# Four-pick or two-pick groups in the expert gathers of a two-block transformer kernel

## What is computed

```python
q = (ht @ w_q).reshape(T, PEER_HEADS, 2, PEER_QDIM // 2)
s = jnp.einsum('thpd,pnd->thpn', q, sub_keys).astype(jnp.float32)
top_s, top_i = lax.top_k(s, PEER_TOPK)
...
best_s, best_j = lax.top_k(cand_s.reshape(T, PEER_HEADS, -1), PEER_TOPK)
experts = jnp.take_along_axis(cand_i.reshape(T, PEER_HEADS, -1), best_j, axis=-1)
gates = jax.nn.softmax(best_s, axis=-1)
...
act = jax.nn.gelu(jnp.einsum('cd,ced->ce', xc, u[ec]))
return jnp.einsum('ce,ced->cd', gc.astype(xc.dtype) * act, v[ec])
```

## Time and profile before

| | |
|---|---|
| median of 3 runs | 2549.35 us (2547.14 to 2553.7) |
| profiled execution, its own time | 2536.68 us |
| its span, first to last instruction | 2534.9 us |
| TensorE busy | 1432.2 us, 56% |
| VectorE busy | 1292.3 us, 51% |
| ScalarE busy | 420.5 us, 17% |
| GpSimd busy | 557.1 us, 22% |
| moved by DMA | 894.91 MB, mean 353 GB/s |
| gathers (L829) | 512, 536.90 MB |
| from the dot of pick 0 to that of pick 255, first and second PEER stage | 736.7 us and 733.8 us |

### The profile page before, as it was taken

How to read it: one execution, slowest core, us unless ns; L and a number is a source line. 1 busy time by engine, 2 the same in 40 slices (tenths; PEclk the granted TensorE clock), 3 DMA queues, 4 the chain that set the end, 5 groups by cost and what they waited for, 6 DMA issues and landing times.

```text
span 2534.9 us, 26747 instructions
## 1 busy us (share of the span) xinstructions
PE 1432.2 (56%) x10223; PEld 744.0 (29%) x10223; DVE 1292.3 (51%) x3307; ACT 420.5 (17%) x1218; POOL 557.1 (22%) x571
## 2 busy tenths in 40 slices
PE   6998666766797845442333333699674333233334
PEld 4665333433574623110000000465442100000000
DVE  2622000100465566877555555484766776555555
ACT  1152000000214312231100000123323231000000
POOL 1000000000001133333333333100333333433332
PEclk9999877888898978665555565899887655556556
DMA  9988999999984678888999999892798889999998
GB/s 388 407 254 343 427 429 429 428 429 427 331 336 169 223 295 344 335 339 326 379 388 390 393 391 387 337 371 93 309 377 330 322 324 366 386 388 406 392 398 338
DMA packets 147200, 894.91 MB, mean 353 GB/s; under 512 B 18460, under 2 KB 30588, under 8 KB 63868
## 3 DMA queue, kind: packets, MB, share of 16 engines
q0 software_dynamic: 73728, 536.90, 53.4%
q1 hardware_dynamic: 73340, 356.25, 35.5%
HBM read 889.68 MB, written 3.42 MB: 352 GB/s over the span
## 4 chain that ended last, share of the span: by engine, by line
DMA 37%; PE 29%; DVE 17%; issue 6%; POOL 6%; ACT 5%; SPq 1%; POOLq 0%; DVEq 0%; PEldq 0%; ACTq 0%
DMA sb_area<-in_peer_uv,sb_peer_e 22%; DMA sb_area<-in_moe_w_gu 13%; PE psum L2055 8%; POOL sb_area L829 6%; DVE sb_area L2841 5%; PE psum L1394 5%; PE psum L1403 3%; PE psum L1480 3%; PE psum L1694 2%; DVE sb_area L2816 2%; ACT sb_peer_e L1188 2%; DMA sb_area<-in_ada_w 1%; PE psum L1719 1%; PE psum L1984 1%; DVE sb_area L2753 1%
## 5 line engine op out<-in xcount | busy, mean ns | idle before, releaser
L2055 PE MATMUL psum<-sb_area 128*32 128x512 f32 x2048 | 450.6, 1009 | 877.0 <-DVE sb_area L2816 877.0
L829 POOL DMA_INDIRECT sb_area<-in_peer_uv,sb_peer_e x512 | 538.8, 1052 | 1199.7 <-PE psum L2055 822.5
L2841 DVE CUSTOM_DVE_ANT_0 sb_area<-sb_area 128x1024 f32<-128x1024 f32 x448 | 547.7, 1224 | 417.9 <-DMA sb_area<-in_peer_uv,sb_peer_e 408.6
L2055 PEld LDWEIGHTS psum<-sb_area 128*32 128x32 f32 x2048 | 77.1, 155 | 1207.8 <-DVE sb_area L2816 1022.1
L1694 PE MATMUL psum<-sb_area 128*32 128x256 f32 x2048 | 173.5, 513 | 129.7 <-DMA sb_area<-in_moe_w_gu 127.2
L2335 DVE COPY sb_area<-psum 128x128 f32<-128x128 f32 x32 | 9.3, 292 | 392.2 <-PE psum L1706 392.2
L1278 ACT ACTIVATE sb_small<-sb_small 128x4 f32<-128x4 f32 (+1 forms) x134 | 27.5, 205 | 1092.8 <-DVE sb_small L2841 1092.4
L1394 PE MATMUL psum<-sb_area 128*128 128x256 f32 x784 | 174.6, 384 | 4.6 <-DVE sb_area L2169 3.2
L807 POOL TENSOR_SCALAR_AFFINE_SELECT sb_area<-sb_area 128x256 f32<-128x256 f32 x1 | 0.4, 406 | 726.2 <-DVE sb_area L2639 726.2
L1394 PEld LDWEIGHTS psum<-sb_area 128*128 128x128 f32 x784 | 150.0, 192 | 28.6 <-DVE sb_area L2169 3.5
L2250 DVE SCALAR_TENSOR_TENSOR sb_area<-sb_area,sb_c_silu 128x2048 f32<-128x2048 f32 x49 | 115.2, 2350 | 70.6 <-DMA sb_area<-in_ada_w 68.6
(11 more groups left out here) (380 smaller groups left out, 1629.6 us busy)
## 6 DMA issues: line engine op xcount, KB each, us to landing
sb_area<-in_moe_w_gu SPq DMA_DIRECT2D x30, 4096.0 KB, 33.6
sb_area<-in_ada_w SPq DMA_DIRECT2D x72, 1024.0 KB, 12.9
sb_area<-in_moe_w_dn SPq DMA_DIRECT2D x32, 2048.0 KB, 24.2
sb_area<-in_peer_w_q SPq DMA_DIRECT2D x8, 2048.0 KB, 8.8
sb_area<-in_sb_w_in SPq DMA_DIRECT2D x6, 2048.0 KB, 21.4
sb_area<-in_odd_w_in SPq DMA_DIRECT2D x6, 2048.0 KB, 10.7
sb_area<-in_even_w_in SPq DMA_DIRECT2D x5, 2048.0 KB, 14.9
sb_area<-in_moe_w_gu SPq DMA_DIRECT2D x4, 2048.0 KB, 20.7
```

What stands on the lines that cost most here:

```text
L829: pool.indirect_dma_start(uv_rows[s], None, rows, bass.IndirectOffsetOnAxis(ap=peer_e[:, m:m + 1], axis=0)).then_inc(named(f"uv_loaded{s}" ...
L2055: last = pe.matmul(ps[BLOCK * b:BLOCK * (b + 1), 4 + 2 * t + half, :], diag[:, s, :], uv_rows[s][:, D + half * HALF:D + (half + 1) * HALF] ...
L2841: dve.tensor_tensor_reduce(uv_rows[s][:, 0:D], uv_rows[s][:, 0:D], h_rep[m // P][m % BLOCKS][:, :], 1.0, 0.0, ALU.mult, ALU.add, dots[:, m ...
```

## The change

Only one number is changed. Every place that uses BATCH follows it.

```diff
@@ -55,7 +55,7 @@
 BLOCK = 32
 BLOCKS = P // BLOCK
 BODY = 32
-BATCH = 4
+BATCH = 2
 UNIT = 32
 UNITS = T // UNIT
```

## The result

| | before | after |
|---|---|---|
| median of 3 runs | 2549.35 us | 2451.76 us (2451.54 to 2453.15) |
| ratio of the two | | 0.9616, 95% interval 0.9594 to 0.9638 |
| profiled execution, its span | 2536.68, 2534.9 us | 2451.54, 2449.8 us |
| TensorE, VectorE, ScalarE busy | 56%, 51%, 17% | 68%, 53%, 18% |

The change made the kernel 3.8% faster. The forecast was 2472 us with a range of 2450 to 2502, so the result lies 1.8 us inside the lower end.

A forecast was written before the change was run, and what follows sets the result against it. Waits bound the kernel: late landings in the free stretch, VectorE stopped by ScalarE's detours in the searches. -47.0 - 29.0 - 4.6 + 2 = -78.6, rounded to -77, gave about 2460 us profiled and a 2472 us median, range 2450 to 2502.

The forecast's parts named there:

- The free stretch: Picks 112 to 255 of both PEER stages, no search running: 2.51 us a pick for 2.67, together -47.0 us.
- lead: How long before the last queued landing GpSimd issues the next group; to rise from 4.0 to 9.3 us.
- The search stretches: Picks 28 to 111 of both PEER stages, 14-pick stretches with one search each: 41.7 us a stretch, together -29.0 us.
- Picks 8 to 27: In both PEER stages, with projection on TensorE in picks 16 to 23: -2.3 us per stage, together -4.6 us.
- Ends: First eight picks of a stage called even, the last single waits about 1 us: +2 us for both.
- Between the stages: From the first PEER stage's last dot to the second's first; the prediction had no term for it.
- From the profiled execution to the median: Profiled execution forecast at about 2460 us, the median taken 12.7 us above it as before: 2472 us.
- Half the gain: Rival, chance 0.15: longer search stalls, stretches of 44 us, 2.55 us a pick in the free stretch; -39, 2510 us.
- Transfers full already: Rival, chance 0.05: 2.67 us a pick stays, searches bring -29 at best or nothing; 2520 to 2549 us.
- TensorE the bound: Rival, chance 0.04: a pair's matmuls don't run side by side, 6.9 us a pair at half clock; 2770 us.
- detour: ScalarE's `move_picks` and `move_gates` for each search; VectorE's gelu waits behind it put at 8.1 us in all searches.
- start + 7: Pick, counted from a search's start, where ScalarE's detour falls; with pairs always a group's last, so fully waited for.

The follow-up runs named there:

- ring of 6: The changed kernel (pairs) with 6 slots in place of 8; 2573.99 us, ratio 1.0135 to the kernel before.
- ring of 4: The changed kernel (pairs) with 4 slots in place of 8; 3097.58 us, ratio 1.2184 to the kernel before.
- quads and added matmuls: The kernel before, groups of four, with 20 unread matmuls behind each group's weighing from pick 112 on; 2526.6 us, ratio 0.9928.
- singles: The changed kernel with every pick its own group (BATCH = 1 in place of 2); 2493.41 us, ratio 0.9796 to the kernel before.

## Why the prediction was right

**The free stretch** (-47.0 predicted, -46.9 measured). The step from landings to lead to pace held in each number: a turn of 5.2 to 6.4 us at the half clock where 5.6 was worked out, a lead of 9.3 on average there (8.3 to 10.6) for 9.3, a pace of 2.507 and 2.513 for 2.51, and 416 GB/s for "about 410". One yardstick in it was too short: a lead of 3.1 us (5.6 less 2.5) was said to cover an issue, by which the 4.0 us of before would have been enough. The lost time there shows that about 5.5 us are needed; with 9.3 us it made no difference. The ring of 6 shows that it is the queued picks, not the pieces, and the ring of 4 that still fewer of them cost far more, 1.22 times the time of before.

**The search stretches** (-29.0 predicted, -32.6 measured). The waits came as said, 5.3 and 2.8 us, nearly all stretches alike, landings gone. The forecast of 41.7 us was 0.5 too high for most, which took 41.2: two more gelu round trips of 0.27 us were counted and one showed, and VectorE took 32.8 us without its waits where 33.1 was the mean of before. The stretch of picks 42 to 55 took 42.4 and 41.8 us.

**Picks 8 to 27** (-4.6 predicted, -6.1 measured): right in sign and near in size. Of its terms, the pair that has to share TensorE with the projection took 5.49 us there for the 5.5 worked out. What it costs was priced at 2 us and is more. ScalarE's copy of the projection waits for TensorE (first stage), and with it the gelu of picks 24 and 25 and VectorE, 4.3 us in the first stage and 4.5 in the second, where quads had no such wait:

```profile
954.09 1.02 ACT L997 ACTIVATE sb_area<-psum 128x1024 f32<-128x1024 f32 x1 [10.05 <-PE psum L1974]
```

VectorE's waits for landings, which fell from 15.2 to 4.4 us in the first stage, made up for it.

**Ends** (+2 predicted, -5.5 measured). This step failed in its reading, "even". It counted the work of TensorE for the first eight picks and not when the first slots come free. Nearly all of it, 4.8 us, is in the second stage. There the kernel after issues the ninth gather 13.8 us behind dot 0, where it was 20.5 before (19.9 for 20.9 in the first stage):

```profile
1764.61 0.94 POOL L829 DMA_INDIRECT sb_area<-in_peer_uv,sb_peer_e  x1 [23.12 <-PE psum L2055]
```

Dot 8 waits for nothing now, while it stood 4.88 us in the earlier trace rows: slots come free earlier, as in the free stretch, in a place that the prediction left out. At the tail nothing was lost; from dot 255 of the second stage to the end it is 12.0 us in both.

**Between the stages** (0 predicted, +6.1 measured) is the disturbance shown above, not seen in this size in other kernels with pairs. It happens to undo the 5.5 us of the ends. That the sum of -77 came within 9 us of the measured -85 is in part this luck: two terms of 6 to 8 us that were missed, with opposite signs.

**From the profiled execution to the median.** By the terms, the profiled execution was forecast at 2460 and took 2451.54 us. The other 12 us of the miss of 20 are the assumption that the new median would lie 12.7 us above the profiled execution again. The lower end of the range does not follow from the values named for it: 2.49 us a pick and 41 us a stretch give 2458 by the same sum, and the result of 2451.76 lies below that. That it lies inside 2450 is not owed to the working. The kernel before ran between 2537 and 2554 us, here and beside the experiments; the kernel after had three runs within 1.6 us. Its pace is set by a queue that never runs short, and that of before by 50 late landings that come more or less late; that this makes the scatter is argued, not shown.

**The rivals.** *Half the gain*: the stretches did not go to 44 us. *Transfers full already*: before, 389 GB/s; after, 416 over 358 us. The Trainium skill (DMA: Bandwidth & Descriptors, Where 436 GB/s comes from) puts a core's share of HBM at about 358 GB/s. The trace disagrees for this read pattern on a core that runs alone, with 389 GB/s before and 416 after; no run here has a second core at work. *TensorE the bound*: a pair took 3.63 us at the half clock as expected, and 43 of 120 ran at the full one; the mean clock of the free stretch was 0.78 where it had been 0.58.

## What to carry to other kernels

In a ring of prefetched slots, measure the lead: how long before the last queued landing the next transfer is issued. It is the picks still queued times the pace, less the time from landing to release; smaller groups raise it mostly by the first factor, and once it is above what an issue needs (5.5 us here) neither a higher clock nor still smaller groups bring more. Below that it is a guide and not a law: one kernel here had leads near 4 us at little loss.

An engine's detour costs by where it falls in the group. After a change of the group size, look at each fixed position again (start + 7 had been the last pick for some searches only), and then at what the moved one now collides with: such moves, by one or two picks each, brought another 55 us of median here after the 98 of the change (51 between the profiled executions, of which 6 are the disturbance between the stages).

When a stage has two limits, such as detour waits and landing waits, look at each stretch by itself. In some neither remedy alone showed anything (42.0 us became 42.1 or 42.4) and both together brought 4.2 us; in others either one brought most of the gain. The sum over all stretches (26.4, 32.6 and 60.1 us) shows neither.

## What the runs showed of the hardware

- Two pairs of weighing matmuls in different column groups, 16 records, took 3.75 us at the half clock when issued back to back, against 3.63 us for one pair (8 records): matmuls further back in the program run beside the ones ahead if their column groups are free.
- A gather that was issued 5.5 us or more before the last queued landing was hardly late (0.17 us at most on average), though its transfer takes 2.49 us. By the latency of 5.6 us into an idle queue a lead of 3.1 us should do; but with 4 to 4.5 us it still came 0.6 to 1.0 us late in most kernels, and 0.2 us in the one with quads and added matmuls.
- With the queue always full, 9 to 11 of the 286 gaps in the two free stretches are still 2.9 to 4.1 us long (kernels with pairs or singles). Two of them, behind pick 144 of each stage, are VectorE's own work (L2418 and L2419, 1.22 us each) and are made up by the next two dots. The others are late landings, each about 1 us. In the second stage of the kernel after they come behind picks 148, 184 and 220, every 36 picks (90.7 us), and with singles every 32 (80.6 us). At each of these three the trace has a DMA packet of 8 KB of the kind "instruction" on queue 14, which takes 0.33 us and starts 2.1 us before the late dot; with singles it is the same. Other such packets are not followed by a late landing (at 2342.1 and 2355.1 us, say), so that they make the gaps is argued, not shown.
- The granted clock of the free stretch, a mean that mixes its two levels, 1.2 GHz (0.5) and 2.4 GHz (1.0), was 0.58 with quads, 0.78 with pairs, 0.87 with quads and added matmuls, and 1.00 with singles. Each of the last three gave TensorE more matmul time there than quads did.
